# Cached latent pages laid down in four column planes and turned on VectorE, in a one-core decoder step

## The reference, cut to what matters

```python
def page_step(carry, inp):
    phys, j = inp
    c_blk = cache_ckv[layer, phys]            # 128 x 256
    kpe_blk = cache_kpe[layer, phys]          # 128 x 32
    pos = j * page + jnp.arange(page, dtype=jnp.int32)
    k = _mla_keys(c_blk, kpe_blk, pos, w_uk, g_k)   # rmsnorm of [c @ w_uk | kpe], rotated
    sc = jnp.einsum('bthd,bphd->bhtp', q, k).astype(jnp.float32) * MLA_SCALE
    return _online_update(carry, sc, c_blk), None   # softmax, and p @ c_blk
...
carry, _ = lax.scan(page_step, init, (page_table.T, jnp.arange(n_pages, dtype=jnp.int32)))
```

## Time and profile before

| | us |
|---|---|
| median of 3 runs | 2971.61 |
| lowest, highest | 2969.59, 2974.54 |
| the profiled execution, span from its first to its last instruction | 2969.8 |
| TensorE busy in it | 2921.2 (98%) |
| VectorE busy | 1585.4 (53%) |
| ScalarE busy | 1040.5 (35%) |
| GpSimd busy | 331.3 (11%) |

### The profile page before, as it was taken

How to read it: one execution, slowest core, us unless ns; L and a number is a source line. 1 busy time by engine, 2 the same in 40 slices (tenths; PEclk the granted TensorE clock), 3 DMA queues, 4 the chain that set the end, 5 groups by cost and what they waited for, 6 DMA issues and landing times.

```text
span 2969.8 us, 55923 instructions
## 1 busy us (share of the span) xinstructions
PE 2921.2 (98%) x20229; PEld 1778.4 (60%) x20229; DVE 1585.4 (53%) x3545; ACT 1040.5 (35%) x2177; POOL 331.3 (11%) x467
## 2 busy tenths in 40 slices
PE   7999999999999999999999999999999999999999
PEld 4676677755555555555466667766555555555554
DVE  3666665655655555554146566666556555555531
ACT  1333333333444444442023333344244444444410
POOL 1110000011111111110010001000211111111100
PEclk9999999999999999999999999999999999999999
DMA  7000000023122222223520000000412222122322
GB/s 273 32 17 17 17 17 17 14 59 106 50 59 59 57 56 55 61 79 114 197 95 17 17 17 24 11 17 14 134 51 55 55 58 59 50 63 53 104 87 82
DMA packets 192165, 179.56 MB, mean 60 GB/s; under 512 B 93769, under 2 KB 171666, under 8 KB 189842
## 3 DMA queue, kind: packets, MB, share of 16 engines
q1 hardware_dynamic: 190144, 175.18, 19.3%
q10 hardware_dynamic: 1746, 0.81, 0.1%
HBM read 153.41 MB, written 22.50 MB: 59 GB/s over the span
## 4 chain that ended last, share of the span: by engine, by line
PE 89%; DVE 7%; ACT 2%; issue 1%; DMA 0%; POOL 0%; SPq 0%; DVEq 0%; ACTq 0%
PE ps L1856 30%; PE ps L1440 12%; PE ps L1949 7%; PE ps L1872 4%; PE ps L1843 4%; PE ps L1674 4%; PE ps L1885 4%; PE ps L1434 3%; PE ps L1699 2%; PE ps L1639 2%; PE ps L1451 2%; PE ps L1446 2%; PE ps L1874 2%; ACT U L664 1%; PE ps L1646 1%
## 5 line engine op out<-in xcount | busy, mean ns | idle before, releaser
L1325 DVE TENSOR_REDUCE w_in<-w_in 128x8 f32<-128x512 f32 x512 | 351.3, 686 | 548.3 <-ACT w_in L821 544.9
L1856 PE MATMUL ps<-w_uk,region 128*128 128x512 f32 x1248 | 586.0, 597 | 0.8
L821 ACT ACTIVATE w_in<-ps 128x512 f32<-128x512 f32 x512 | 305.7, 597 | 213.2 <-PE ps L1856 198.2
L1440 PE MATMUL ps<-w_in,xT 128*128 128x256 f32 (+6 forms) x1360 | 378.3, 431 | 0.6 <-DVE xT L940 0.4
L1856 PE MATMUL ps<-w_uk,xT 128*128 128x512 f32 x800 | 378.0, 600 | 0.5
L1856 PEld LDWEIGHTS ps<-w_uk,region 128*128 128x128 f32 x1248 | 216.1, 191 | 190.4 <-issue 189.9
L1440 PEld LDWEIGHTS ps<-w_in,xT 128*128 128x128 f32 (+1 forms) x1360 | 246.4, 185 | 111.4 <-issue 69.3
L538 POOL TENSOR_TENSOR rs<-us,mhalf 128x1 f32<-128x1 f32 (+4 forms) x132 | 130.9, 991 | 1366.9 <-DVE us L978 729.0
L1856 PEld LDWEIGHTS ps<-w_uk,xT 128*128 128x128 f32 x800 | 139.5, 192 | 124.3 <-issue 124.3
L1843 PEld LDWEIGHTS ps<-ident,region 128*128 128x128 f32 x960 | 116.2, 141 | 110.8 <-issue 106.3
L800 ACT COPY region<-ps 128x512 f32<-128x512 f32 x156 | 91.3, 585 | 251.5 <-PE ps L1843 250.3
(11 more groups left out here) (401 smaller groups left out, 4132.3 us busy)
## 6 DMA issues: line engine op xcount, KB each, us to landing
region<-in_cache_ckv SPq DMA_DIRECT2D x480, 128.0 KB, 2.0
w_in<-in_w_in SPq DMA_DIRECT2D x16, 1240.0 KB, 11.1
mix_rows<-xn SPq DMA_DIRECT2D x16, 512.0 KB, 2.9
region<-in_cache_kpe SPq DMA_DIRECT2D x512, 16.0 KB, 1.8
region<-in_w_out SPq DMA_DIRECT2D x8, 1024.0 KB
xt<-in_x_prompt SPq DMA_DIRECT2D x11, 512.0 KB, 4.2
xt<-x_mid SPq DMA_DIRECT2D x11, 512.0 KB, 4.4
region<-in_w_mem_kv SPq DMA_DIRECT2D x2, 2048.0 KB, 24.1
```

The source lines that it names most:

```text
L821: tell(act.activation(sqb[:, j % 2, :], ps[:, 2 + j % 2, :], ACT.Square), s.pkn_sq, np_)
L1325: tell(dve.tensor_reduce(pst[:, 0, j * H:j * H + H], heads(sqb[:, j % 2, :], H), X, ALU.add), s.pkn_red, np_)
L1440: ins = mm(out, xT[:, k, 0:T], w_in[:, k, c0:c0 + w], start=k == 0, stop=k == KD - 1)
L1856: ins = mm(ps[:, 2 + j % 2, :], page[:, o_:o_ + P], w_uk[:, c, :], start=c == 0, stop=c == 1)
```

## The change

Two HBM buffers are added. While the prompt tiles run, SyncE copies every page of the layer from its place in the cache to `lsc`, HBM to HBM, in four planes: plane i has columns 64*i to 64*i+63 of the page's 128 rows, 256 B to a row. It copies the positional keys of a page to `ksc`. This is `gather_pages`, four groups (32 pages, 64 transfers) to each of the eight tiles, between the store of the latent rows and the store of the mix; a single wait on `gathered` for all 512 transfers stands ahead of the first load from these buffers. In the page stage SyncE loads, for each group, the planes twice four pages at a time (`load_quarters`: partition 32*i+q gets rows 4q to 4q+3 of plane i, 1 KB), the positional keys in one transfer (`load_kpe`), and the eight pages in their own layout as before, for the values (`load_pages`, into a ring of two groups instead of four).

VectorE turns a pair of pages in one instruction, 32x32 blocks of each of the four partition quarters (`turn_quarters`), straight into `pcT`, which has six places instead of five. After it, partition p of chunk c has latent column 2p+c, so `w_uk`, `w_uv` and the turns of the new tokens' latents and of the accumulators use the same interleaved order (`pairs`, `chunk`). TensorE's `turn_pair` and ScalarE's `copy_pair` are gone. `w_out` is loaded from group 24 on; from group 20 the pages go to another part of SBUF.

```diff
+        lsc = nc.dram_tensor("pages_by_quarter", [DEPTH, DB * PAGES, 4, P, R // 4], F32).ap()
+        ksc = nc.dram_tensor("pages_kpe", [DEPTH, DB * NG, P, G * ROPE], F32).ap()
...
+                def gather_pages(k):
+                    for j in range(G):
+                        i = k * G + j
+                        v = sp.value_load(ptab[0:1, i:i + 1], min_val=0, max_val=POOL - 1)
+                        sp.dma_start(lsc[L, i],
+                                     a["cache_ckv"][L, bass.ds(v, 1)].rearrange("o p (i x) -> i (o p) x", i=4)).then_inc(s.gathered, 16)
+                        sp.dma_start(ksc[L, k, :, j * ROPE:(j + 1) * ROPE],
+                                     a["cache_kpe"][L, bass.ds(v, 1)].rearrange("o p r -> (o p) r")).then_inc(s.gathered, 16)
+                def load_kpe(k):
+                    if k >= 2:
+                        sp.wait_ge(s.kpe_rot, L * DB * NG + k - 1)
+                    sp.dma_start(kpr[:, k % 2, :], ksc[L, k]).then_inc(kpe_in[k % 2], 16)
+                def load_quarters(k, h):
+                    if k:
+                        sp.wait_ge(s.pcT_ready, (L * DB * NG + k - 1) * (G // 2) + 2 * h + 2)
+                    i = k * G + h * (G // 2)
+                    sp.dma_start(quarters_of(k, h).rearrange("p (j n) -> p j n", j=G // 2),
+                                 lsc[L, i:i + G // 2].rearrange("j i (q u) x -> (i q) j (u x)", u=4)).then_inc(low_in[h], 16)
...
                         sp.wait_ge(s.o_ps, TP * (L + 1))
                         sp.dma_start(sinp, a["c_sinp"]).then_inc(s.x_in, 16)
-                        load_pages(0)
+                        sp.wait_ge(s.gathered, 16 * 2 * DB * PAGES * (L + 1))
+                        load_quarters(0, 0)
+                        load_kpe(0)
+                        load_quarters(0, 1)
+                        load_kpe(1)
...
+                    for k in range(4 * t, 4 * t + 4):
+                        gather_pages(k)
                     sp.wait_ge(s.mix_ready, n + 1)
                     sp.dma_start(mix[L, t, 0:T, :], xn[0:T, :]).then_inc(s.mix_out, 16)
...
+                def turn_quarters(k, q):
+                    n, o_ = (L * DB * NG + k) * (G // 2) + q, 2 * R * (q % 2)
+                    dve.wait_ge(low_in[q // 2], 32 + 16 * (L * DB * NG + k + 1))
...
+                    if n >= 6:
+                        dve.wait_ge(s.ps_ps, (n - 6) // (G // 2) + 1)
+                    src = quarters_of(k, q // 2)[:, o_:o_ + 2 * R].rearrange("p (j u r c) -> p j u c r", j=2, u=4, c=2)
+                    tell(dve.transpose(pcT(k * (G // 2) + q).rearrange("p (j c q u) -> p j u c q", j=2, c=2, u=4), src), s.pcT_ready, n)
...
                     for j in range(G):
                         np_ = n0 * G + j
                         sample_step(k, j)
+                        if j % 2 == 0 and j + 2 < G:
+                            turn_quarters(k, j // 2 + 1)
+                        if j == G - 1 and k + 1 < DB * NG:
+                            turn_quarters(k + 1, 0)
...
                 def keys(k, j):
-                    pe.wait_ge(s.pcT_evac, np_ // 2 + 1)
+                    pe.wait_ge(s.pcT_ready, np_ // 2 + 1)
```

More of the change, by code:

```diff
@@ L208, in pcT @@
         def pcT(q):
[L210 to L211 removed]
+            q %= 6
+            return pairs_r[:, q, :] if q < 3 else (pairs_x[:, q - 3, :] if q < 5 else W[:, 0:512])
         cosp = xn[:, :].rearrange("p (j n) -> p j n", j=PAGES)
@@ L244, in build, with quarters_of, chunk @@
         late = scratch[:, 0:2 * G * RW].rearrange("p (g j n) -> p g j n", g=2, j=G)
+        late_low = scratch[:, 2 * G * RW:2 * G * RW + G * R].rearrange("p (h n) -> p h n", h=2)
+        LATE = 20
         def pages_of(k):
-            return cring[:, k % NG, :, :] if k < DB * NG - 2 else late[:, k - (DB * NG - 2), :, :]
+            return cring[:, k % 2, :, :] if k < LATE else late[:, k % 2, :, :]
+        def quarters_of(k, h):
+            return low[:, h, :] if k < LATE else late_low[:, h, :]
+        def chunk(ap, c):
+            return ap.rearrange("p (r c) -> p c r", c=2)[:, c, :]
         qrep = U[0:TS, 0:1024]
@@ L441, in _ @@
                     sp.dma_start(smv[:, :, c, :], mv_src[c]).then_inc(s.smk_in, 16)
[L442 to L447 removed]
+                for k in range(1, DB * NG):
+                    if k == LATE:
+                        sp.wait_ge(s.smo_ps, L + 1)
+                    load_quarters(k, 0)
+                    load_quarters(k, 1)
+                    if k + 1 < DB * NG:
+                        load_kpe(k + 1)
+                    load_pages(k)
+                    if k == 1:
+                        sp.wait_ge(s.st_zero, 2 * L + 2)
+                        for h in range(GH):
+                            sp.dma_start(s_bd[GK * h:GK * h + GK, :, GV * h:GV * h + GV],
+                                         a["state_gla"][L, :, h].rearrange("b k v -> k b v")).then_inc(s.smk_in, 16)
                     if k == 14:
@@ L455, in _ @@
                         sp.dma_start(mix[L, TP, 0:TS, H * VD:D], xs).then_inc(s.mix_out, 16)
-                for g in (2, 3, 0, 1):
-                    sp.wait_ge(s.ring_free, (L + 1) * DB * NG - (2 if g < 2 else NG))
-                    k = g * (KD // NG)
-                    sp.dma_start(w_out[:, k:k + KD // NG, :],
-                                 a["w_out"][L, k * P:(k + KD // NG) * P, :].rearrange("(k p) n -> p k n", p=P)).then_inc(s.w_more_in, 16)
+                    if LATE + 4 <= k < LATE + 4 + NG:
+                        o_ = (k - LATE - 4) * (KD // NG)
+                        sp.dma_start(w_out[:, o_:o_ + KD // NG, :],
+                                     a["w_out"][L, o_ * P:(o_ + KD // NG) * P, :].rearrange("(k p) n -> p k n", p=P)).then_inc(s.w_more_in, 16)
                 sp.wait_ge(s.mix_out, 16 * ((NT + 1) * L + NT))
@@ L694, in _ @@
                         act.wait_ge(s.kqv_ps, 3 * (TP * L + t) + 2)
-                        tell(act.copy(kT[:, :, t * P:t * P + P], ps[0:QK, 0:2, :].rearrange("p c (h n) -> p (c h) n", n=P)), s.kT_evac, TP * L + t)
+                        own(act.copy(kT[:, :, t * P:t * P + P], ps[0:QK, 0:2, :].rearrange("p c (h n) -> p (c h) n", n=P)))
                         act.wait_ge(s.kqv_ps, 3 * (TP * L + t) + 3)
```

105 lines of the change are left out of this document (38 added, 67 removed).

## The result

The changed kernel takes 3519.34 us (median of four runs, 3514.25 to 3524.01) against 2972.98 for the one before, measured beside it: ratio 1.1838, 95% interval 1.1822 to 1.1854. It is slower, as forecast, by 546 us instead of the 740 of the sum; the range holds it. The profiled execution has a span of 3522.2 us against 2969.8.

The account below looks back on a forecast made before the run. The prediction took TensorE, busy 98% of the span, as the bound. From 2969.8 us it added 427 and 413 for late first keys, subtracted 100 saved, giving 3710, about 3712 us as median; range 3060 to 4340.

Parts of the forecast that it names:

- the rivals that had a chance: Prompt-tile copies: four engines at one-way price, 3067 us (0.28); four engines, all doubled, 4333 us (0.22); copies hidden, 2883 us (0.06).
- The copies themselves: Prompt tiles, the deciding term: page copies on 4 DMA engines take 125.5 us a tile, delaying first keys by 427 and 413 us.
- The price of a piece: Prompt-tile copies: a 256 B piece copied HBM to HBM costs 28 ns, between 18.5 and 37 ns.
- SyncE's issuing: Prompt tiles: a page with its key takes SyncE 1.6 us, 51 us a tile; tile 2's rows some 12 us late, rest hidden.
- turning point of 64: Prompt tiles: the copies hide where a tile's DMA queue falls below 64 us, the shortest tile.
- It just fits: Page stage: VectorE's tightest turn ends before TensorE wants the pair, with 0.1 to 0.4 us left.
- VectorE's 10 us: Page stage: allowance for `sample_step` work ahead of VectorE's turns, 10 us over two layers, bounds 0 and 25.
- The sign named for this: Page stage: groups taking over 19.5 us would show VectorE late and the 100 us saving oversized.
- The 110 for TensorE's turns: Page stage: taking 256 blocks of turns at 0.43 us off TensorE gains 110 us.
- No cost for the page stage's DMA: Page stage: plane transfers run on 16 engines; nearly twice the bytes raise the DMA share from 0.20 to about 0.4, at no cost.
- the copies hide: Rival for the prompt tiles: all 16 engines share the copies, 40 us a tile, total 2883 us, faster; chance 0.06.
- without a break: Sign in the prompt tiles: DMA at 2 to 3 tenths, four engines of 16, working continuously.

Follow-up runs that it names:

- e4: e3 with the source's rows in the outermost place of each page copy instead of the four planes; 3035.7 us, ratio 1.0225.
- e3: The kernel before, plus the changed kernel's copies into the two HBM buffers, which nothing reads, and the wait for them; 3591.49 us, ratio 1.2095.
- e5: The changed kernel with each page's copy split into two transfers of two planes each; 4383.46 us, ratio 1.4743.
- e11: e10 with the page copies in four planes again, as in the changed kernel, but without key copies; 2935.61 us, ratio 0.9885.
- e10: e9 with the earlier VectorE turns of e7; 2880.71 us, ratio 0.9698.
- e7: e1 with each VectorE turn placed a step or two earlier; 2954.07 us, ratio 0.9929.
- e1: The changed kernel with the page copy written with its rows outermost instead of its four planes; 2977.03 us, ratio 1.002.
- e9: e6 with SyncE's page-stage queue reordered: second half-group of columns no longer behind page loads that wait for a ring slot; 2918.89 us, ratio 0.983.
- e6: e1 without key copies: keys loaded in the page stage straight from the cache, into a ring of three groups; 3217.38 us, ratio 1.0815.
- e2: The changed kernel with each page copied as it lies, 16 pieces of 8 KB, so attention uses misplaced latents; 2963.69 us, ratio 0.9977.

## Why the prediction was right, and where it was wrong

**Direction and range: right, but not by the term that was to decide.** The sum has the tiles wait for four DMA engines. The runs show four engines, and a loss that is SyncE's queue. The time lies in the range by luck: the two errors below go against each other, and the rivals that had a chance all vary the engines' term alone. What stands is the number of engines in "The copies themselves": level 72 GB/s in planes, 36 with two planes, over 200 with the rows first, and e4 against e3 puts 556 us on nothing but the order of a copy's dimensions. That they are always the same, which was taken without evidence, e5 bears out for the two transfers of a page, and e11, where page follows page at a level of 72 to 74 GB/s, for successive pages. The Trainium skill's rule ("DMA: Bandwidth & Descriptors", "Why a DMA increments its semaphore by 16 and not by 1"), that the largest k up to 16 dividing both slowest dimensions counts, is what these levels agree with.

**The price of a piece: wrong.** The step took 28 ns, because each byte is read from and written to HBM. In e11 a piece is under way for 18.0 ns, the lower end and no more than a store of the earlier trace rows; but an engine takes a new one every 14.1 ns. The reading went wrong at the rows: busy share times span over packets is how long a packet lasts, and sums over packets that overlap. So the forecast's price is twice the real one, and even the lower bound of 18.5 is too high. By the Trainium skill's figure for large copies ("DMA: Bandwidth & Descriptors", "Latency and other measured facts") the bytes alone would take 19 ns, an estimate; the trace has 14.1.

**"SyncE's issuing", 1.6 us a page: wrong, and this decides.** The prediction read 1.6 us off loads into SBUF and gave SyncE 51 us a tile, under the engines' 125.5. Measured: 2.0 us a page when the copies run on 16 engines, 3.3 when they go in planes, 105 us a tile. The engines need 58, and 64 with pauses (e11). With the right price the prediction's own sum for a tile is 58 + 3.3 + 6.1 = 67 us, an estimate, just above its own turning point of 64: it would have said that the copies all but hide, some 2883 us, and been wrong by over 600. The term that was thought hidden under the engines lies above them. The forecast's 125.5 against 109.4 is two errors that partly cancel, a price of twice the real one and an issue of half of it. The mix store, issued behind the copies, lands 4.0 us after its issue (2.9 in e10, 5.0 in e11): the engines have no backlog worth 50 us, the waiting is in SyncE's queue. Behind this step the first keys came at 979.6, not 1092 (+314.5 for +427; layer 1 +304.3 for +413).

**"It just fits", VectorE's 10 us: too small.** With 0.1 to 0.4 us of slack reckoned for turns up to 1.05 us, and 1.10 measured, the slack was gone, and the sample's steps stand ahead of some turns. What late turns cost, the pairs that differ in their place alone show: e7's page stages are (678.5 - 668.9) + (681.5 - 666.6) = 24.5 us shorter than e1's, e10's 37 us shorter than e9's, at the upper bound of 25 and beyond it. The saving was 67 to 72 instead of 100. The sign named for this came: a group over 19.5 us (19.9, from 1200.76 to 1220.70 between the turns of the maxima, L1935). The 110 for TensorE's turns was about right: with the turns early, e10's page stages are 52.5 + 47.3 = 100 us shorter than before.

**No cost for the page stage's DMA: right.** Its share went from 0.25 to 0.38 in the whole stage (0.42 in e10's, where TensorE idles 8 us in 660).

**The rival "the copies hide", 2883 us: as a time it is reachable, not by its mechanism alone.** With 16 engines the price of SyncE's queue is left (e1: 2977), as the prediction's own 12 us for tile 0 hinted, with 1.6 where 2.0 holds: +42 and +29.5 in the tiles. Only with the key copies gone and the turns early is the kernel at 2880.71.

**Signs named beforehand.** TensorE at 5 to 8 tenths and DMA at 2 came about as said; "without a break" did not, and just there the wrong step could be seen: at 0.25 us a slice the four engines stop after every page.

**What stays open.** Why SyncE's instructions become longer when a copy in planes is in flight (the value load 0.27 to 0.70, the key copy 0.50 to 1.13). In this the engines may come in after all. In e5, with half as many engines and twice the pieces on each, the key copy's issue takes 1.6 us. That fits an issue that waits until the copy ahead leaves room. The Trainium skill ("Perfetto Trace Analysis", "DMA Instruction — HWDGE (DVE, Sync)") says that the time shown for a DMA instruction runs from the moment its semaphores are met, over the wait for the descriptor generator and the making of the descriptors, to the end of the increments that the sequencer itself adds to the semaphore, and that there can be more descriptors than their buffer holds. The lengthened issues agree; but the value load is no DMA instruction and isn't explained by this, and no run here separates the causes. Nor was a copy issued from another engine's queue tried.

## What to carry to other kernels

A copy that is to hide under other work has two bills, the engines' and the issuing queue's, and the longer of them counts. Read the first from the level of GB/s that a steady stretch holds, not from the duration of a packet. Read the second from the durations of that queue's instructions in the kind of transfer that will be used: a stretch in which the engines run empty between transfers while the queue has no gap is bound by the queue. For the layout, put a long dimension outermost on both sides: here it was worth 556 us at the same bytes. Before a load that may wait for a free buffer, issue what is needed sooner (e6 against e9: 298 us); and place a turn a product ahead, not just in time (e7).

## What the runs showed of the hardware that was not expected

- Issuing a copy from HBM to HBM takes SyncE 0.49 to 0.55 us against 0.33 for a page's load into SBUF, and the size of its pieces hardly counts: 0.49 with 16 pieces of 8 KB in e2, 0.55 with 512 of 256 B in e1. In planes it takes 0.72.
- A value load on SyncE lasts 0.27 us beside copies on 16 engines and 0.70 to 0.73 beside copies in planes.
- A piece of 256 B copied within HBM lasts 18.0 ns, as a store from SBUF does, but in a steady stretch an engine takes one every 14.1 ns: packets of one engine overlap, so their summed durations overstate what it is loaded with.
- VectorE's turn of 128x512 fp32 elements in 32x32 blocks takes 1.10 us, strided or not, 1.6 times a sum over as many elements (0.69).
- TensorE's idle time is paid twice: 95 us more of it in e6's page stage came with 57 us more of busy time, at a granted clock of 0.91 for 0.99.
